# All eight chunks of the experts' gate and up product as split products; GpSimd makes the row numbers

## The reference

```python
def route(h, w_r, bias):                     # per token: 8 of 64 experts and their weights
    scores = jax.nn.sigmoid(h @ w_r)
    ...
    return eidx, w

def body(acc, blk):                          # one block of tokens of one expert
    tok, wt, e = blk
    xb = h_pad[tok]
    a = jax.nn.silu(xb @ w_gate[e]) * (xb @ w_up[e])
    yb = (a @ w_down[e]).astype(jnp.float32) * wt[:, None]
    return acc.at[tok].add(yb), None
```

## Time and profile before

| | |
|---|---|
| runs | 1163.1 us median of 3 (1159.67 to 1173.99) |
| profiled execution | 1160.63 us, span on the core 1158.9 us |
| mean granted clock of TensorE | 0.965 of full speed |
| busy: PE, DVE, ACT, POOL | 1085.3, 740.9, 641.5, 265.4 us |
| moved by DMA | 303.25 MB, mean 262 GB/s |
| chain that ended last | PE 79%, DMA 12%, DVE 5% |

### The profile page before, as it was taken

One profiled execution on the slowest core, in us unless ns is written; L12 is line 12 of the kernel. 1 busy time (PEld: TensorE's weight loads), 2 busy tenths in 40 slices (PEclk: granted clock), 3 DMA queues, 4 the chain that ended last, 5 costly groups with the idle time before them and its releaser, 6 DMA issues.

```text
span 1158.9 us, 17553 instructions
## 1 busy us (share of the span) xinstructions
PE 1085.3 (94%) x5968; PEld 810.0 (70%) x5968; DVE 740.9 (64%) x1322; ACT 641.5 (55%) x848; POOL 265.4 (23%) x180
## 2 busy tenths in 40 slices
PE   6999999898879998999999999999999999999981
PEld 5998459897449886566666666666666666666661
DVE  5734625533834344288888888888877877778852
ACT  4383423333633121267777777777776666766663
POOL 1003210000000100233333333333333333333320
PEclk8999999899989789999999999999999999999995
DMA  9403405332991512399999999999999999999935
GB/s 309 194 1 115 153 35 219 139 152 87 350 327 49 218 75 109 109 335 361 357 365 361 364 362 356 360 365 362 369 366 357 351 361 367 372 368 363 344 96 165
DMA packets 65494, 303.25 MB, mean 262 GB/s; under 512 B 12711, under 2 KB 15347, under 8 KB 40870
## 3 DMA queue, kind: packets, MB, share of 16 engines
q1 hardware_dynamic: 50254, 266.15, 60.4%
q0 software_dynamic: 15200, 36.55, 12.9%
HBM read 285.53 MB, written 34.04 MB: 276 GB/s over the span
## 4 chain that ended last, share of the span: by engine, by line
PE 79%; DMA 12%; DVE 5%; ACT 2%; issue 1%; SPq 1%; DVEq 0%; POOLq 0%; ACTq 0%
PE pair L1780 20%; PE pair L176 17%; PE pair L1812 14%; PE pair L1793 9%; DMA regC<-in_exp_w_up 8%; PE pair L1567 5%; PE pair L1765 4%; PE pair L1470 3%; DMA regA<-q_rows 2%; PE pair L1725 2%; PE pair L1692 1%; DMA regB<-in_xa_wo 1%; DVE regL L1080 1%; DMA regA<-in_w_in 1%; PE pair L1800 1%
## 5 line engine op out<-in xcount | busy, mean ns | idle before, releaser
L1780 PE MATMUL pair<-w_hi,h_parts 128*96 128x512 f32 x768 | 267.7, 430 | 0.0
L705 POOL DMA_INDIRECT acc_rows<-regL x64 | 94.5, 1476 | 396.5 <-ACT regL L1002 213.0
L1812 PE MATMUL pair<-w_hi,act_parts 128*96 128x512 f32 x512 | 165.6, 405 | 8.1 <-DVE act_parts L1417 7.9
L1780 PEld LDWEIGHTS pair<-w_hi,h_parts 128*96 128x96 f32 x768 | 121.5, 165 | 69.7 <-issue 33.9
L696 POOL DMA_INDIRECT regL<-h_rows,regL x65 | 140.8, 2167 | 102.7 <-DVE regL L1287 75.3
L176 PE MATMUL pair<-h_hi,w_parts 128*128 128x260 f32 x640 | 132.0, 288 | 3.8 <-DVE h_lo L1074 3.5
L1002 ACT ACTIVATE regL<-pair,regL 96x1024 f32<-96x1024 f32 x64 | 71.0, 1110 | 113.4 <-PE pair L1812 113.4
L1379 DVE TENSOR_TENSOR lo_A<-regA,w_hi 128x1536 fp32r<-128x1536 f32 x64 | 111.8, 1748 | 0.0
L957 ACT CAST w_hi<-regA 128x1536 fp32r<-128x1536 f32 x64 | 94.6, 1481 | 30.1 <-DMA regA<-in_exp_w_up 23.7
L176 PEld LDWEIGHTS pair<-h_hi,w_parts 128*128 128x128 f32 x640 | 105.3, 193 | 4.8 <-issue 3.0
L1812 PEld LDWEIGHTS pair<-w_hi,act_parts 128*96 128x96 f32 x512 | 80.1, 166 | 37.4 <-issue 5.6
(11 more groups left out here) (322 smaller groups left out, 2096.1 us busy)
## 6 DMA issues: line engine op xcount, KB each, us to landing
regA<-in_exp_w_gate SPq DMA_DIRECT2D x32, 1024.0 KB, 11.0
regA<-in_exp_w_up SPq DMA_DIRECT2D x32, 1024.0 KB, 21.6
regA<-in_exp_w_down SPq DMA_DIRECT2D x32, 1024.0 KB, 23.6
regB<-in_exp_w_down SPq DMA_DIRECT2D x32, 1024.0 KB, 23.7
regB<-in_exp_w_gate SPq DMA_DIRECT2D x16, 1024.0 KB, 11.6
regB<-in_exp_w_up SPq DMA_DIRECT2D x16, 1024.0 KB, 22.8
regC<-in_exp_w_gate SPq DMA_DIRECT2D x16, 1024.0 KB, 10.6
regC<-in_exp_w_up SPq DMA_DIRECT2D x16, 1024.0 KB, 24.0
```

Source lines behind the costliest of these rows:

```text
L705: pool.indirect_dma_start(acc_rows, bass.IndirectOffsetOnAxis(ap=kept[0:SLOTS, r, 0:1].bitcast(U32), axis=0), yX[r][0:SLOTS, :], None, bou ...
L1780: ins = pe.matmul(out, x, w, start=False, stop=half == 1 and k == CUT_K - 1 and s == 2, skip_group_check=True)
L1812: ins = pe.matmul(pair[2][0:SLOTS, h, :], act_parts[:, x, k, :], w[:, k, cols], start=k == 0 and s == 0, stop=k == KF - 1 and s == 2)
```

## The change

- `WHOLE_K`, `gate_up_whole` and `hX` go; `CUT_K` is 4, so both halves of `gate_up` have four chunks, all split. The first matmul now starts the sum, and the product waits at its start for the residue of the turned rows (`turned_d`) and the gate (`act_b`).
- `WG_hi` grows to two buffers of 4096 elements; `WD_hi` moves out of `w_hi` into `wd_parts`, which lies on the former `rows`, so ACT waits for the first sums to land before it goes on behind `turn(0)`.
- The addition of 1024 (L1287) and the copy to `kept` (L1399) go from DVE to POOL: the first into `gather`, with a new tile `idx`; the second, as two copies, into `keep` ahead of `scatter`. DVE's `slots` waits for `kept_ready` instead of POOL's former `rows_left`; PE's `slots` waits for `summed`.

```diff
-WHOLE_K = 2
-CUT_K = (KD - WHOLE_K) // 2
+CUT_K = KD // 2
...
+        with nc.sbuf_tensor("unused_L4", [P, 4160], F32), nc.sbuf_tensor("wd_parts", [P, KF * D], F32R) as wd_parts:
...
+        idx = view(regL, 8816, RING)
-        hX = view(regL, 12024, WHOLE_K, SLOTS)
...
-        WD_hi = view(w_hi, 3072, KF, D)
+        WD_hi = view(wd_parts, 0, KF, D)
...
@@ POOL
+            pool.sem_inc(kept_ready, RING)
             def gather(g, r, b):
                 pool.wait_ge(turned, b + (1 + RING - PAIR))
+                pool.wait_ge(summed, b + 1)
+                pool.sem_inc(clear, 1)
+                pool.tensor_scalar(idx[0:SLOTS, r:r + 1].bitcast(U32), sums[0:SLOTS, r, 0:1], float(FAR), None, ALU.add).then_inc(idx_ready, 1)
                 pool.wait_ge(idx_ready, b + 1)
                 pool.sem_inc(clear, 1)
                 pool.indirect_dma_start(gath[g][0:SLOTS, :], None, h_rows,
-                                        bass.IndirectOffsetOnAxis(ap=sums[0:SLOTS, r, 0:1].bitcast(U32), axis=0),
+                                        bass.IndirectOffsetOnAxis(ap=idx[0:SLOTS, r:r + 1].bitcast(U32), axis=0),
...
+            def keep(r, b):
+                pool.tensor_copy(kept[0:SLOTS, r, 0:1].bitcast(U32), idx[0:SLOTS, r:r + 1].bitcast(U32))
+                pool.tensor_copy(kept[0:SLOTS, r, 1:2], sums[0:SLOTS, r, 1:2]).then_inc(kept_ready, 1)
...
             def step_of_block(i, j, peeled=False):
                 b = i * RING + j
                 gather((j + 1) % PAIR, (j + 1) % RING, b + 1)
                 if not (peeled and j < 2):
+                    keep((j - 2) % RING, b - 2)
                     scatter((j - 2) % RING, b - 2)
@@ ACT
             def turn(b):
                 a.wait_ge(turned, b + (1 + RING))
-                a.copy(hX[:, :, :], pair[1][:, :, 0:SLOTS])
-                a.copy(h_parts[:, 0], pair[1][:, :, SLOTS:(1 + CUT_K) * SLOTS]).then_inc(turned_a, 1)
+                a.copy(h_parts[:, 0], pair[1][:, :, 0:CUT_K * SLOTS]).then_inc(turned_a, 1)
...
             turn(0)
+            a.wait_ge(sums_landed, 16 * NTT)
@@ DVE
             def slots(r, b):
                 v.wait_ge(slots_made, b + 1)
+                v.wait_ge(kept_ready, b + (RING - 3))
                 v.tensor_reduce(sums[0:SLOTS, r, :], ...).then_inc(summed, 1)
-                v.wait_ge(summed, b + 1)
-                v.tensor_scalar(sums[0:SLOTS, r, 0:1].bitcast(U32), sums[0:SLOTS, r, 0:1], float(FAR), None, ALU.add).then_inc(idx_ready, 1)
...
-            def keep(r, b):
-                v.wait_ge(rows_left, b + (1 + RING))
-                v.tensor_copy(kept[0:SLOTS, r, :].bitcast(U32), sums[0:SLOTS, r, :].bitcast(U32)).then_inc(kept_ready, 1)
@@ PE
-            def gate_up(r, b, half):
+            def gate_up(r, b, half, first=False):
                 pe.wait_ge(wg_lo, 2 * b + half + 1)
                 if half == 0:
                     pe.wait_ge(turned_d, b + 1)
+                    if not first:
+                        pe.wait_ge(act_b, b + RING)
...
-            def gate_up_whole(r, b, q, first=False):
...
-                gate_up_whole(j, b, i, first=peeled and j == 0)
-                gate_up(j, b, 0)
+                gate_up(j, b, 0, first=peeled and j == 0)
```

More of the change, by code:

```diff
@@ L226, in sem @@
             return ctx.enter_context(nc.semaphore(name))
-        with nc.sbuf_tensor("w_hi", [P, 8192], F32R) as w_hi:
+        with nc.sbuf_tensor("w_hi", [P, 8320], F32R) as w_hi:
             pass
@@ L255, in trunk @@
         with nc.sbuf_tensor("unused_L", [P, 4160], F32), nc.sbuf_tensor("h2_lo", [P, KD, NT], F32R) as h2_lo:
+            pass
+        with nc.sbuf_tensor("unused_L4", [P, 4160], F32), nc.sbuf_tensor("wd_parts", [P, KF * D], F32R) as wd_parts:
             pass
@@ L393, in trunk @@
         WD_lo = [view(lo_A, 4096, KF, D), view(lo_A, 10240, KF, D), view(lo_B, 4096, KF, D), view(lo_B, 6144, KF, D)]
-        WG_hi = [view(w_hi, 5120, 2, 2, CUT), view(w_hi, 0, 2, 2, CUT)]
-        WD_hi = view(w_hi, 3072, KF, D)
+        WG_hi = [view(w_hi, 4160, 2, 2, CUT), view(w_hi, 0, 2, 2, CUT)]
+        WD_hi = view(wd_parts, 0, KF, D)
         yf = view(regA, 0, NTT, D)
@@ L431, in trunk @@
         silu_done, gated, routed = sem("silu_done"), sem("gated"), sem("routed")
-        h_stored, sums_landed, rows_left, clear = sem("h_stored"), sem("sums_landed"), sem("rows_left"), sem("clear")
+        h_stored, sums_landed, clear = sem("h_stored"), sem("sums_landed"), sem("clear")
         masked, row_table = sem("masked"), sem("row_table")
@@ L729, in _ @@
             for left in (2, 1):
+                keep(RING - left, n_turns * RING - left)
                 scatter(RING - left, n_turns * RING - left)
@@ L955, in cut_up @@
                     a.wait_ge(wg_in[r], q * 32 + 32)
-                k0 = WHOLE_K + half * CUT_K
+                k0 = half * CUT_K
                 a.copy(WG_hi[r % 2][:, half], WG[r][:, :, k0 * FE:(k0 + CUT_K) * FE]).then_inc(wg_hi, 1)
@@ L1389, in _ @@
             n_turns = turns(v)
-            for ahead in (act_b, kept_ready):
-                v.sem_inc(ahead, RING)
+            v.sem_inc(act_b, RING)
             onehot_(0)
@@ L1395, in _ @@
                 onehot_(t + 1)
-            def keep(r, b):
-                v.wait_ge(rows_left, b + (1 + RING))
-                v.tensor_copy(kept[0:SLOTS, r, :].bitcast(U32), sums[0:SLOTS, r, :].bitcast(U32)).then_inc(kept_ready, 1)
             def turn(b):
                 v.wait_ge(turned_a, b + 1)
-                v.tensor_tensor(h_parts[:, 1], pair[1][:, :, SLOTS:(1 + CUT_K) * SLOTS], h_parts[:, 0].bitcast(F32),
+                v.tensor_tensor(h_parts[:, 1], pair[1][:, :, 0:CUT_K * SLOTS], h_parts[:, 0].bitcast(F32),
                                 ALU.subtract).then_inc(turned_d, 1)
@@ L1427, in step_of_block @@
                 if two:
-                    keep((j - 2) % RING, b - 2)
                     cut_down((j - 2) % RING, b - 2)
@@ L1441, in _ @@
             last = n_turns * RING - 1
-            keep(RING - 2, last - 1)
             cut_down(RING - 2, last - 1)
@@ L1445, in _ @@
             gate(last)
-            keep(RING - 1, last)
             cut_down(RING - 1, last)
@@ L1745, in _ @@
             shared_down(2)
-            pe.wait_ge(idx_ready, 1)
+            pe.wait_ge(summed, 1)
             slots(1)
@@ L1763, in turn @@
                 for k in range(KD):
-                    h, n = (k, 0) if k < WHOLE_K else ((k - WHOLE_K) // CUT_K, 1 + (k - WHOLE_K) % CUT_K)
+                    h, n = k // CUT_K, k % CUT_K
                     ins = pe.transpose(pair[1][:, h, n * SLOTS:(n + 1) * SLOTS], g3[0:SLOTS, k, :], ident[0:SLOTS, 0:SLOTS])
                 ins.then_inc(turned, 1)
-            def gate_up(r, b, half):
+            def gate_up(r, b, half, first=False):
                 out = pair[0][0:SLOTS, 0, :].rearrange("p (s f) -> p s f", s=2)
@@ L1778, in gate_up @@
                     x_hi, x_lo = (h_parts[:, x, half, k * SLOTS:(k + 1) * SLOTS] for x in range(2))
-                    for s, (x, w) in enumerate(((x_hi, hi[:, :, k, :]), (x_lo, hi[:, :, k, :]), (x_hi, lo[:, :, WHOLE_K + kk, :]))):
-                        ins = pe.matmul(out, x, w, start=False, stop=half == 1 and k == CUT_K - 1 and s == 2,
+                    for s, (x, w) in enumerate(((x_hi, hi[:, :, k, :]), (x_lo, hi[:, :, k, :]), (x_hi, lo[:, :, kk, :]))):
+                        ins = pe.matmul(out, x, w, start=kk == 0 and s == 0, stop=half == 1 and k == CUT_K - 1 and s == 2,
                                         skip_group_check=True)
@@ L1820, in step_of_block @@
                 b = i * RING + j
-                pe.wait_ge(idx_ready, b + 2)
+                pe.wait_ge(summed, b + 2)
                 slots(b + 2)
-                gate_up_whole(j, b, i, first=peeled and j == 0)
-                gate_up(j, b, 0)
+                gate_up(j, b, 0, first=peeled and j == 0)
                 if not (peeled and j == 0):
```

2 lines of the change are left out of this document (removed).

## The result

The changed kernel takes 1198.5 us (median of 4 runs, 1197.7 to 1203.8) beside 1168.2 for the kernel before on the same chip: ratio 1.0275 [1.0192, 1.0359]. That is slower, clear of the noise, but the lower end of the interval lies just under the 2% from which a verdict is given, so by that rule it stays unclear. Ratios leave out executions that took over 1.5% more than the fastest of the same kernel, medians count all, and a ratio need not be the quotient of the two medians. The profiled execution is 1198.32 us with a span of 1196.5, against 1160.63 and 1158.9: +37.7 us.

A forecast was written before the change was run, and what follows sets the result against it. Transfers were taken to run at their limit, PE a hair slower. Then 62 steps of 10.7, 663.4 less 623.8, give +39.6; with +1 for the start, +40.6 on 1160.6: 1201 us, range 1174 to 1226.

The forecast's parts named there:

- One-block loop: Down subtraction, POOL's copies, ACT's scaling, next down-weight cut: 7.75 + 1.01 + 1.92 = 10.7 us per block, setting the pace.
- the copies behind the second half: POOL's two copies to `kept` wait for the second gate-up subtraction's end, then take 0.38 + about 0.06.
- Two-block loop: PE, ACT and DVE through the turned rows' residue: 20.8 us for two blocks, 10.4 per block.
- rival 1: POOL's copies do not wait, so steps are 10.4 through DVE's residue: 1183 us, chance 0.26.
- ACT's scaling idle until POOL's copy and not until PE: Sign in the profile after: ACT's scaling waits for POOL's copy, not PE's down product; otherwise the One-block loop was wrong.
- the fullest engine: Sign in the profile after: DVE would be the busiest engine, with PE idle once per block.
- Rival 2: Gathered rows land late for PE's turn, every second block losing 0.7: +22, 1223 us, chance 0.07.
- Start: ACT waits for first sums to land before its cuts, delaying the second block's cuts: +1 us, bounds 0 and 2.5.
- DMA share below 0.98: Sign in the profile after: longer steps delay SP's loads, so transfers fall below their limit, the share under 0.98.
- rival 3: DVE's longer subtractions cost less than 2.0 each, transfers still set steps of 10.06: 1161 us, chance 0.12.
- rival 4: PE's saving of 0.42 per block arrives, 9.56 per block or the transfers' own limit: 1135 us, chance 0.05.
- DVE's own 9.8: DVE's work alone needs 9.8 us per block, so no loop can be shorter; held against rival 4.

The follow-up runs named there:

- the kernel with the cover alone: Changed kernel with PE's gate-up products reordered, those with cast rows first, so matmuls cover the wait for DVE's residue: 1194.5 us, ratio 1.028.
- the split product alone: Changed kernel with the row-number addition and the copy to `kept` back on DVE, all eight chunks still split: 1193.1 us, ratio 1.027 to the kernel before.
- With the cover and without the wait at the start: The split product alone, plus cast-row products first and ACT's wait for the stores removed: 1159.9 us, ratio 0.998 to the kernel before.
- the last kernel of the experiments: The split product alone, plus cast-row products first and DVE's expert register load issued ahead, ACT's start wait kept: 1161.8 us, ratio 1.002.

## Why the prediction held, point by point

- **Size and sign.** 1201 against 1198.5; on the profiled execution +40.6 against +37.7. Steps gave 33.2 where I had 39.6, the start 5.5 where I had 1, the end -1.0 where I had 0: two errors of opposite sign, so that a total right to 2.5 us is in part luck.
- **One-block loop, the pace I took.** Right in its links, shown by the kernel with the cover alone, and 0.2 too long: 10.49 (7.46 + 0.09 + 1.01 + 1.93) where I had 10.7. The mis-sized term is the copies behind the second half. I priced both at 0.19 and a hand-over; but the first is under way when the subtraction ends and ends with it, and only the second (0.17) follows. The Trainium skill, "SBUF — State Buffer", Who interferes with whom, says that a DVE instruction with two SBUF inputs contends with a GpSimd instruction that reads SBUF, and that one with at most one SBUF input, outside DVE's two-port modes, does not; the rows agree, 1.6 to 1.7 beside the subtraction and 0.17 beside the residue, which reads PSUM.
- **Two-block loop, rival 1.** I had it 0.3 below the other loop. It is 10.50, for PE takes 9.87 where I had 9.67: the first half behind the wait is 3.01 for twelve matmuls, not 2.76. So the rival's loop was as long as the one forecast: its 10.4 was 0.1 too low, and my 10.7 was 0.2 too high. With the late start it costs 1193 us by itself (the split product alone), some 6 of the missing 10 us for the step and 4 for the start. So the copies were not needed for the loss, though they suffice for it (1194.5 with the cover). "ACT's scaling idle until POOL's copy and not until PE" came out mixed, 20 times to 39, as two loops that tie would give. DVE is not the fullest engine either: PE still is, 36.9 to DVE's 33.7.
- **Rival 2, late gathers**, came in part. The gather starts 0.82 behind the addition's end, where I had put it at once; rows are late in 20 blocks, for some 0.1 per step on the mean (10.60 less the 10.50 of either loop).
- **Start.** Sized 1, bounds 0 and 2.5; measured 5.5. Of this 0.5 lies ahead of the loop, where nothing changed (ACT has its first turned rows at 483.81 instead of 483.35), and 5.0 between there and the first scaling. I named the wait for the stores, which costs nothing; the experiments say the lost cover, with PE idle and the clock that falls in the idle time.
- **Transfers.** "DMA share below 0.98" was wrong: 1.01 in both windows. And the ground for it, that they ran at their limit before, does not hold. The share hardly moves while the landing of a weight load falls from 21.6 to 9.7 us (DMA issues of before and after):

```profile
regA<-in_exp_w_up SPq DMA_DIRECT2D x32, 1024.0 KB, 21.6
```

```profile
regA<-in_exp_w_up SPq DMA_DIRECT2D x32, 1024.0 KB, 9.7
```

  With the cover and without the wait at the start the first window moves 368 GB/s, more than the 358 of the earlier trace rows, and the last kernel of the experiments moved 370, as shown above; 358 at a share of 1.02 was not the limit:

```profile
719.20:759.00 39.80, 39.73 (x210) 28.48 (x209) 36.74 (x45) 31.24 (x29) 18.10 (x8) 1.00 1.02 368
```

- **Rivals 3 and 4** need the loops to be short; with the cover they are, and then the time is rival 3's 1161 (1158.6 and 1159.9), not rival 4's 1135. Both of the obstacles that I gave for rival 4 were misread. The transfers did not stop at 358. DVE's own 9.8 was measured at 9.92, but it is no floor, as I had it: 0.7 of it is the register load, and with that issued ahead blocks take 9.65. Rival 3's sum is a little off too: with its 2.0 per subtraction the 20.8 falls by twice 0.29, to 20.2 and not 20.1.

## What to carry to other kernels

Work that is dropped from the fullest engine may have been the cover for another engine's result: look at what its first instruction waits for once it is gone, and reorder the products so that those with early inputs stand first (here 1193 to 1159 us). A tiny operation given to GpSimd beside DVE's two-input subtractions costs the rest of that subtraction, so ask what is queued behind it and not how long it is. When two loops have the same length, taking away one shows nothing; test each in the absence of the other.

## What was not expected of the hardware

- A GpSimd operation whose span has begun need not get its reads in ahead of a DVE subtraction that begins later: the second copy started 0.26 before it (810.13 against 810.39) and still ended 0.04 behind it, and much the same in 61 blocks of that kernel. The copy took 0.17 to 2.58 us by its place alone. The same page of the Trainium skill ("SBUF — State Buffer", Who interferes with whom) lets issue order decide who blocks; by the starts in these rows it did not here, though spans on POOL are rough.
- The gather's issue stands 0.82 behind an addition on its own engine that it waits for. Where the addition was DVE's and long done, it starts 0.31 behind the scatter ahead of it on POOL.
- A DMA share of 1.0 does not say that no more would fit: 345 GB/s with landings of 9.7 us, 358 with 21.6 and 370 in the last kernel of the experiments all read 1.01 to 1.02.
